# The SSM step sizes behind the convolution, the first loads in another order, and 64 products of a zeroed tile

## The reference, cut to what matters

```python
u = rmsnorm(x, mix_pre_g[0])                      # 256 x 1024
z, xbc, dt = split(u @ w_in, [2048, 5120], -1)    # w_in: 1024 x 5152; dt: 32 columns, the step sizes
xbc = silu(depthwise_conv4(xbc, conv_w) + conv_b) # 3072 channels
xs, bm, cm = split(xbc, [2048, 2560], -1)
dt = softplus(dt + dt_bias);  a = -exp(a_log)     # 32 heads
y = ssd(xs, dt, a, bm, cm)                        # scan; needs cumsum(dt * a)
y = (y + d_skip * xs) * silu(z);  y = grouped_rmsnorm(y) * norm_g;  h = y @ w_out
mem_n = rmsnorm(mem, mem_norm_g)                  # for the cross attention after it
...
```

## Time and profile before

| | us |
|---|---|
| median of 3 runs | 981.83 (981.80 to 982.46) |
| the profiled execution | 982.02 |
| its span, first to last instruction | 980.2 |
| its mean granted TensorE clock | 0.983 of full |

### The profile page before, as it was taken

One profiled execution on the slowest core, in us unless ns is written; L12 is line 12 of the kernel. 1 busy time (PEld: TensorE's weight loads), 2 busy tenths in 40 slices (PEclk: granted clock), 3 DMA queues, 4 the chain that ended last, 5 costly groups with the idle time before them and its releaser, 6 DMA issues.

```text
span 980.2 us, 15470 instructions
## 1 busy us (share of the span) xinstructions
PE 927.5 (95%) x6560; PEld 855.4 (87%) x6560; DVE 562.7 (57%) x644; ACT 487.9 (50%) x669; POOL 37.3 (4%) x52
## 2 busy tenths in 40 slices
PE   2899998998999999999999999999999599999996
PEld 2899997876899889999988899997898499999885
DVE  4778654784475475455544755765654645554533
ACT  4555747773464564443343644665645534444332
POOL 1000001220000000000000021000000000000000
PEclk9899999998999999999999999999999799999999
DMA  9465553223464265555555697433543445555551
GB/s 294 141 194 187 172 173 109 88 86 131 170 221 166 86 215 172 178 195 183 172 188 198 197 275 236 131 129 123 198 152 98 139 133 193 188 171 175 201 181 43
DMA packets 120917, 163.80 MB, mean 167 GB/s; under 512 B 4060, under 2 KB 106644, under 8 KB 120868
## 3 DMA queue, kind: packets, MB, share of 16 engines
q1 hardware_dynamic: 117396, 151.47, 47.4%
q0 software_dynamic: 3472, 11.63, 4.0%
HBM read 162.01 MB, written 1.07 MB: 166 GB/s over the span
## 4 chain that ended last, share of the span: by engine, by line
PE 85%; DVE 7%; ACT 3%; DMA 2%; issue 2%; SPq 0%; POOL 0%; DVEq 0%
PE bank L433 77%; DMA w_raw<-in_ssm_w_in_dram 2%; DVE w_lo L1110 2%; DVE ntmp L1171 1%; PE bank L713 1%; PE bank L684 1%; DVE x L1174 1%; PE bank L533 1%; DVE ntmp L1150 1%; ACT ntmp L822 1%; PE bank L610 1%; PE bank L768 1%; DVE stats L1139 0%; DVE stats L1141 0%; PE bank L758 0%
## 5 line engine op out<-in xcount | busy, mean ns | idle before, releaser
L1110 DVE TENSOR_TENSOR w_lo<-w_raw,w_hi 128x2048 fp32r<-128x2048 f32 x136 | 310.8, 2290 | 229.2 <-ACT w_hi L802 229.1
L433 PE MATMUL bank<-actT_hi,w_hi 128*128 128x256 f32 x1280 | 365.5, 286 | 4.7 <-DVE dtc L1217 2.0
L433 PE MATMUL bank<-actT_lo,w_hi 128*128 128x256 f32 x1280 | 363.8, 284 | 0.0
L433 PE MATMUL bank<-actT_hi,w_lo 128*128 128x256 f32 x1280 | 363.6, 284 | 0.0
L802 ACT ACTIVATE w_hi<-w_raw 128x2048 fp32r<-128x2048 f32 x136 | 258.7, 1907 | 118.3 <-DMA w_raw<-in_ffn_w_down_dram 54.8
L433 PEld LDWEIGHTS bank<-actT_hi,w_hi 128*128 128x128 f32 x1280 | 247.3, 193 | 6.5 <-issue 4.2
L433 PEld LDWEIGHTS bank<-actT_lo,w_hi 128*128 128x128 f32 x1280 | 247.4, 193 | 0.1
L433 PEld LDWEIGHTS bank<-actT_hi,w_lo 128*128 128x128 f32 x1280 | 247.3, 193 | 0.0
L433 PE MATMUL bank<-w_lo,hT_hi 128*128 128x512 f32 x176 | 70.2, 399 | 0.0
L433 PE MATMUL bank<-w_hi,hT_hi 128*128 128x512 f32 x176 | 69.4, 394 | 0.0
L433 PE MATMUL bank<-w_hi,hT_lo 128*128 128x512 f32 x176 | 69.0, 392 | 0.0
(11 more groups left out here) (208 smaller groups left out, 1300.7 us busy)
## 6 DMA issues: line engine op xcount, KB each, us to landing
w_raw<-in_ffn_w_gu_dram SPq DMA_DIRECT2D x44, 1024.0 KB, 5.1
w_raw<-in_ffn_w_down_dram SPq DMA_DIRECT2D x22, 1024.0 KB, 4.9
w_raw<-in_ssm_w_in_dram SPq DMA_DIRECT2D x20, 1024.0 KB, 5.3
w_raw<-in_mem_w_kv_dram SPq DMA_DIRECT2D x16, 1024.0 KB, 5.6
w_raw<-in_ssm_w_out_dram SPq DMA_DIRECT2D x8, 1024.0 KB, 4.9
w_raw<-in_mem_w_q_dram SPq DMA_DIRECT2D x8, 1024.0 KB, 5.2
w_raw<-in_mem_w_o_dram SPq DMA_DIRECT2D x8, 1024.0 KB, 4.9
w_raw<-in_w_kv_dram SPq DMA_DIRECT2D x8, 1024.0 KB, 5.7
```

Source lines behind the costliest of these rows:

```text
L433: ins = pe.matmul(dst, a, b, start=first and n == 0, stop=last and n == len(passes) - 1, skip_group_check=True)
L1110: dve.tensor_tensor(lo[:, s, :], raw[:, s, :], hi[:, s, :].bitcast(F32), ALU.subtract).then_inc(w_lo_done, 1)
```

## The change

- **SP's order** becomes x (two), `pre_row` (taken from POOL), the identity alone (64 KB of the constants), unit 0, the four small parameter loads, unit 1, the rest of the constants, units 2 and 3, `dtw`, then units 4 onward.
- **POOL** waits until the first half of u is written before it loads the dt rows and the table, and until three units are used before the 2 MB of memory gain, `mem` and `post_row`.
- **TensorE** first waits for a zeroed tile (`cum3`, bfloat16), then multiplies it 40 times with 256 columns, then needs the identity only; 24 more such products follow the transposes of the parameters. The first 40 and the 24 are loops (`WARM`). Unit 0 no longer waits for `dt_biased`.
- **The step sizes**: `dtw_hi` and `dtw_lo` are made after the convolution loop; the 24 matmuls stand behind z0, the two transposes behind z1 (banks 6 and 7), `turn(1)` waits for `dt_biased`. ScalarE's table load, memory statistics and the Abs, Exp, Ln, Exp, Ln chain move together to behind the Silu of z2, VectorE's part with them.
- **Unit 0** is made in halves on ScalarE and VectorE. ScalarE's first change of table stands between units 0 and 1. VectorE does the constants (L1193 to L1199) after unit 1's lo instead of ahead of the turn, and waits for the parameters before the turn.
- With one bank entry fewer, `z` and later units swap banks 0 and 1. The buffers from `phase` on move up by 96 bytes, to a multiple of 128.

```diff
+WARM = [10, 6]
...
-BANKED = [("params", 0), ("dt", 0)] + [n for n in NAME_OF if KIND[n[0]] != "M"]
+BANKED = [("params", 0)] + [n for n in NAME_OF if KIND[n[0]] != "M"]
...
+        phase = -(-at[0] // 128) * 128
...
+        dt_heads = place("dt_heads", [P, S], F32, phase + 44544)
...
             for t in range(ST):
                 sp.dma_start(x[:, t, :], A["x"][0, t * P:(t + 1) * P, :]).then_inc(x_loaded[t], 16)
-            sp.dma_start(const[:], A["consts"][:, 0:C_HOT]).then_inc(const_loaded, 16)
+            sp.dma_start(pre_row[:], every_row(TURN_GAIN[0])).then_inc(pre_first, 16)
+            sp.dma_start(const[:, 0:P], A["consts"][:, 0:P]).then_inc(ident_loaded, 16)
+            load(0)
             sp.wait_ge(par_cleared, 1)
             sp.dma_start(par_rows[0:TAPS * CT, 0, :], A["ssm_conv_w"][0].rearrange("k (c p) -> (k c) p", p=P)).then_inc(par_loaded, 16)
             sp.dma_start(par_rows[0:CT, 1, :], A["ssm_conv_b"][0].rearrange("(c p) -> c p", p=P)).then_inc(par_loaded, 16)
             sp.dma_start(par_rows[G_ROW:G_ROW + XT, 1, :], A["ssm_norm_g"][0].rearrange("(c p) -> c p", p=P)).then_inc(par_loaded, 16)
             sp.dma_start(d_pair[D_ROW:D_ROW + XT, :], A["ssm_d"][0].rearrange("(c e) -> c e", e=2)).then_inc(par_loaded, 16)
-            sp.dma_start(dtw[:], row_tiles(w_in, 0, KD, DI + CONV, SSM_HEADS)).then_inc(par_loaded, 16)
-            for u in range(NUNITS):
+            load(1)
+            sp.dma_start(const[:, P:C_HOT], A["consts"][:, P:C_HOT]).then_inc(const_loaded, 16)
+            for u in range(2, SLOTS):
+                load(u)
+            sp.dma_start(dtw[:], row_tiles(w_in, 0, KD, DI + CONV, SSM_HEADS)).then_inc(dtw_loaded, 16)
+            for u in range(SLOTS, NUNITS):
                 load(u)
...
-            pool.dma_start(pre_row[:], every_row(TURN_GAIN[0])).then_inc(pre_loaded, 16)
+            pool.wait_ge(u_ready, 1)
...
             pool.wait_ge(u_ready, 2)
+            pool.wait_ge(w_used, 3)
             pool.dma_start(pre_row[:], every_row(TURN_GAIN[1])).then_inc(pre_loaded, 16)
 
             pool.dma_start(memV[:], mem_t).then_inc(mem_loaded, 16)
...
-            pe.wait_ge(const_loaded, 16)
+            def warm(n):
+
+                with pe.Fori(0, n):
+                    for _ in range(4):
+                        pe.matmul(bank[:, 2, 0:S], cum3[:, 0:P], cum3[:, 0:S], start=True, stop=True, skip_group_check=True)
+
+            pe.wait_ge(zeros_made, 1)
+            warm(WARM[0])
+            pe.wait_ge(ident_loaded, 16)
             turn(0)
...
             pe.wait_ge(consts_made, 1)
             for r in range(2):
-                ins = pe.transpose(bank[:, 0, r * P:(r + 1) * P], par_rows[:, r, :], ident)
+                ins = pe.transpose(bank[:, 3, r * P:(r + 1) * P], par_rows[:, r, :], ident)
             ins.then_inc(par_turned, 1)
+            warm(WARM[1])
             turn_done(0)
...
-            pe.wait_ge(dtw_lo_done, 1)
-            for k in range(KD):
...
+            def steps():
+
+                pe.wait_ge(dtw_lo_done, 1)
+                for k in range(KD):
+                    ins = product(bank[0:SSM_HEADS, 6, 0:S],
+                                  [(dtw_hi[:, k, :], actT_hi[:, k, :]), (dtw_hi[:, k, :], actT_lo[:, k, :]), (dtw_lo[:, k, :], actT_hi[:, k, :])],
+                                  k == 0, k == KD - 1)
+                ins.then_inc(dt_mm, 1)
+
+            def steps_turned():
+
+                pe.wait_ge(dt_copied, 1)
+                for t in range(ST):
+                    ins = pe.transpose(bank[:, 7, t * SSM_HEADS:(t + 1) * SSM_HEADS], dt_heads[0:SSM_HEADS, t * P:(t + 1) * P],
+                                       ident[0:SSM_HEADS, 0:SSM_HEADS])
+                ins.then_inc(dt_turned, 1)
...
             u0 = U[("xbc", 0)]
-            pe.wait_ge(dt_biased, 1)
-            pe.wait_ge(t_out["dve"], 1)
...
+                pe.wait_ge(const_loaded, 16)
                 pe.wait_ge(dt_ready, 1)
...
-                banked("z", i, actT_hi, actT_lo, FREED[V_OF[("z", i)] - 4] if i < 2 else None)
+                banked("z", i, actT_hi, actT_lo, FREED[V_OF[("xbc", 9)]] if i < 2 else None)
+                if i == 0:
+                    steps()
+                if i == 1:
+                    steps_turned()
                 if i == 3:
+                    pe.wait_ge(dt_biased, 1)
                     turn(1)
                 if i == 4:
...
-            act.wait_ge(par_loaded, 80)
-            act.activation(dtw_hi[:], dtw[:], ACT.Copy).then_inc(dtw_hi_done, 1)
             turn(0, actT_hi)
+            hi_part(0, 0)
+            hi_part(0, 1)
+            act.preload_act_table_set("silu_and_others")
             hi_upto(1)
...
+            act.wait_ge(t_out["dve"], 1)
...
             done[0] = U[("z", 0)] + 2
+            act.wait_ge(dtw_loaded, 16)
+            act.activation(dtw_hi[:], dtw[:], ACT.Copy).then_inc(dtw_hi_done, 1)
...
                 hi_upto(U[("z", i)] + 2)
+                if i == 1:
+                    act.wait_ge(dt_mm, 1)
+                    act.activation(dt_heads[0:SSM_HEADS, :], bank[0:SSM_HEADS, 6, 0:S], ACT.Copy).then_inc(dt_copied, 1)
                 act.wait_ge(w_used, U[("z", i)] + 1)
...
-                if i == 1:
+                if i == 2:
...
+                    act.wait_ge(dt_biased, 1)
+                    own.mark(act.activation(dtc[:, 2], dtc[:, 1], ACT.Abs))
...
+                    act.activation(dt_row[:, 1, :], dt_row[:, 1, :], ACT.Exp).then_inc(dt_logged, 1)
                     act.wait_ge(dt_ready, 1)
                     act.activation(dtc[:, 3], dtc[:, 4], ACT.Ln).then_inc(dt_ln, 1)
...
+                elif u == 0:
+                    dve.wait_ge((first_hi, w_hi_done)[part], 1)
...
+            dve.memset(one_col, 1.0).then_inc(zeros_made, 1)
...
-            dve.wait_ge(par_loaded, 80)
+            dve.wait_ge(par_loaded, 64)
...
+            dve.tensor_copy(par_rows[d_rows, 1, :].rearrange("c (e n) -> c e n", e=2), d_pair[d_rows, :].unsqueeze(2).broadcast_to([XT, 2, HD])).then_inc(consts_made, 1)
+            turn(0, actT_hi, actT_lo)
+            lo_part(0, 0)
+            lo_part(0, 1)
+            dve.wait_ge(par_turned, 1)
...
+            lo_upto(1)
             dve.wait_ge(const_loaded, 16)
...
+            def steps_biased():
+                dve.wait_ge(dt_turned, 1)
+                dve.wait_ge(rows_loaded, 64)
...
+                dve.tensor_tensor(dtc[:, 1], dt_raw, bias_row, ALU.add).then_inc(dt_biased, 1)
...
+            def steps_ready():
+                dve.wait_ge(dt_logged, 1)
...
             own.n += 2 * per
             done[0] = 14
+            dve.wait_ge(dtw_hi_done, 1)
+            dve.tensor_tensor(dtw_lo[:], dtw[:], dtw_hi[:].bitcast(F32), ALU.subtract).then_inc(dtw_lo_done, 1)
             for i in range(DI // TC):
                 lo_upto(U[("z", i)] + 2)
-                if i == 1:
+                if i == 2:
+                    steps_biased()
                     for t in range(ST):
...
```

More of the change, by code:

```diff
@@ L810, in hi_part @@
                 ins = act.activation(hi[:, u % SLOTS, cols], raw[:, u % SLOTS, cols], ACT.Copy)
+                if u == 0 and part == 0:
+                    ins.then_inc(first_hi, 1)
                 if part:
@@ L928, in _ @@
                         statistic(2 + t, t, memV[:, t, :])
+                    act.wait_ge(dt_biased, 1)
+                    own.mark(act.activation(dtc[:, 2], dtc[:, 1], ACT.Abs))
+                    own.wait()
+                    own.mark(act.activation(dtc[:, 3], dtc[:, 2], ACT.Exp, scale=-1.0))
+                    own.wait()
+                    act.activation(dtc[:, 4], dtc[:, 3], ACT.Ln, bias=one_col)
+                    act.activation(dt_row[:, 1, :], dt_row[:, 1, :], ACT.Exp).then_inc(dt_logged, 1)
                     act.wait_ge(dt_ready, 1)
@@ L1116, in lo_part @@
                 s = u % SLOTS
-                if part == 0:
+                if part == 0 and u:
                     dve.wait_ge(w_hi_done, u + 1)
+                elif u == 0:
+                    dve.wait_ge((first_hi, w_hi_done)[part], 1)
                 ins = dve.tensor_tensor(lo[:, s, cols], raw[:, s, cols], hi[:, s, cols].bitcast(F32), ALU.subtract)
@@ L1233, in _ @@
-            own.wait()
-            for t in range(ST):
-                ins = dve.scalar_tensor_tensor(out=adt3[:, t], in0=dtc[:, 5, t:t + 1, :].broadcast_to([P, 3, SSM_HEADS]), scalar=-1.0,
-                                               in1=dt_row[:, 1:2, :].broadcast_to([P, 3, SSM_HEADS]), op0=ALU.mult, op1=ALU.mult)
-            ins.then_inc(dt_ready, 1)
+            def steps_biased():
+                dve.wait_ge(dt_turned, 1)
+                dve.wait_ge(rows_loaded, 64)
+                own.mark(dve.memset(brows[:, S:3 * P], NEG))
+                bias_row = dt_row[:, 0:1, :].broadcast_to([P, ST, SSM_HEADS])
+                dt_raw = bank[:, 7, 0:ST * SSM_HEADS].rearrange("p (t h) -> p t h", t=ST)
```

(22 more changed lines are left out.)

71 lines of the change are left out of this document (12 added, 59 removed).

## The result

The changed kernel takes 969.35 us (median of 4 runs, 968.44 to 969.64), the kernel before 982.14 beside it: a ratio of 0.9868, interval 0.985 to 0.9885. The gain is 12.8 us where 9.4 was forecast, and the time lies 0.15 under the low end of the range. The profiled execution took 969.12, its span is 967.3 and its mean granted clock 0.986.

A forecast was written before the change was run, and what follows sets the result against it. TensorE, busy 95% of the span, bounds the kernel, so it must begin earlier or do less. 13.9 (head) - 2.8 - 0.15 - 1.6 (z units) = 9.35 off 982.02 gives 972.7, by median 972.5; range 969.5 to 977.0.

The forecast's parts named there:

- the 96 bytes and the swapped banks: Moved buffers and banks: old placing cost ScalarE's Copy nothing, so 0, or a few tenths either way.
- the head: Everything before unit 0: 12.1 us gained, plus 1.79 if unit 0 runs at the full clock level, 13.9 together.
- S: Start of unit 0 on TensorE, forecast at 15.5 us instead of 27.63.
- rival 1 in its mild form: Head's transfers come later: parameters land at 12.8, unit 0 starts at 18.1, kernel takes 975.1; chance 0.20.
- Unit 0's clock: Unit 0 runs at the full clock level, lasting 5.76 us instead of 7.55: 1.79 gained.
- The products: 40 zeroed-tile products before the turn and 24 after: 0 for both loops; transposes alone had raised the clock.
- The turn: Transposes in the head: second half from 10.1 to 11.0 at the full clock level, ending 13.8 at the lower.
- The z units: Additions to TensorE's unbroken stretch: 24 step-size matmuls 2.8 us, `dtw` rounding 0, two small transposes behind z1 0.15.
- The chain behind z2: Memory statistics and step sizes between z2 and z5: z5 begins 16.1 after z2's end, before 14.5; 1.6 us lost.
- Rival 3 (slower): Step-size chain between z2 and z5 delays `dt_ready`; slower kernel if it came after Z + 19.7; chance 0.03.
- the far end of rival 1: Head: unit 1 lands at 22.97 as before, starts 5.9 later, clock falls (1.8): 980.2; chance 0.03.
- from z5 on nothing different from before but the shift: Changed kernel's timeline after z5: expected the same as before, only earlier.

The follow-up runs named there:

- b_al128: Kernel before with only the buffers from `phase` on 96 bytes higher, at a multiple of 128: 975.7 us, ratio 0.9942.
- a_al32: Changed kernel with the buffers from `phase` on back at the old addresses, 32 bytes past a multiple of 128: 974.84 us.
- a_again: Changed kernel unaltered, run again on another occasion beside other versions on one chip: 970.11 us.
- a_par: Changed kernel with the four parameter loads ahead of unit 0 in SP's queue: 968.37 us.
- a_nowarm: Changed kernel without its 64 products of the zeroed tile: 971.49 us.
- b_order: Kernel before with buffers at a multiple of 128 and the new load order (`dtw` still ahead of unit 1), no products or halves: 968.72 us, ratio 0.9863.
- b_early_par: b_early with the small loads, `dtw` among them, ahead of unit 0 in SP's queue: 967.49 us, ratio 0.9844.
- b_early: b_order with ScalarE's copy of the step sizes between the hi of units 0 and 1, VectorE's bias between their lo: 967.68 us, ratio 0.9853.
- a_warm2: Changed kernel with only the 24 products behind the parameters' transposes, the first 40 left out: 970.3 us.
- a_chain: Changed kernel with the Abs to Exp chain ahead of the memory's statistics, `turn(1)` behind z4 and `cumulate` behind z5: 968.69 us.

## Why the prediction was wrong, point by point

- **The step that failed: "the 96 bytes and the swapped banks".** I priced them at 0 or a few tenths by ScalarE's Copy in and out of the moved buffers. That row answers for ScalarE alone. The engine that bounds the kernel reads `hT`, `y` and `oT` there as stationary operand, 816 times, and the mean durations 392 to 412 beside 389 to 395 for `actT` stood in the profile of before, in groups that I did not lay side by side. The term measures 4.9, by the last part of b_al128 and by the medians of the groups; undone in a_al32 it is 5.2. The medians of whole runs, 6.0 and 5.5, also hold landings and falls of the clock. With 4.9 the sum would have been 13.9 - 4.55 + 4.9 = 14.25 and the forecast 967.6: too low by 1.8, because the head was too hopeful. Two errors stood against each other, and that the measured time lies so close under the range is luck.
- **S.** Forecast 15.5, measured 16.91, and 17.63 in a_again. `pre_row` was there at 7.8, not 6.9; the parameters held VectorE until 11.86, where the sum let it go at 10.1. This is rival 1 in its mild form, at about half its price; a_par took the wait away.
- **Unit 0's clock.** 1.79 was forecast, 7.55 - 5.86 = 1.69 measured. Right in the sum.
- **The products.** Their cost was priced at 0, rightly; but the reason given for doing without them was wrong. Rows 15.90 and 18.62 of the earlier trace rows were taken to show that the turn alone raises the clock for what comes after. In a_nowarm, with nothing between turn and unit 0, unit 0 is at the lower level after 3.7 us of idle time, 2.1 us in the median; whether the level had risen and fallen again in that time, or had never risen, no row shows. And the test itself was one throw of several: after the same 18 transposes the matmuls of the step sizes were at the full level from the first in before, b_order and b_early_par, and at the lower one in b_al128 and b_early. For b_al128:

```profile
15.41 0.42 PE L433 MATMUL bank<-actT_hi,dtw_hi 128*32 128x256 f32 x1 [1.32 <-DVE actT_lo L1158]
```

- In a_warm2 nothing but 18 transposes stands ahead of the 24 products; the last two transposes are 0.11 apart, and the products 0.115 from the first on. The rule of the Trainium skill ("TensorE: Matmul & The Clock Gate", Part 4: PE-mode transpose), that the full level doesn't engage for transposes, disagrees with that row and with 15.90 of before; it agrees with b_al128. What decides between them no run here shows.
- **The turn.** Its second half ran at 0.21 for most of its length, 1.69 instead of 1.0. Since VectorE was waiting for `d_pair` meanwhile, part of it was hidden.
- **The z units.** 24 step matmuls: 2.79, forecast 2.8. Ahead of them TensorE waits 0.25 for `dtw_lo`, which had been priced at 0. The two small transposes cost 0.42 (from 94.93, where z1 begins, to 106.87, where z2 ends, are 11.94, and two units take 11.52), forecast 0.15. Together 3.5, forecast 2.95.
- **The chain behind z2.** Z is the end of z2, here 106.87; z5 begins at Z + 16.1 as forecast, Z + 14.5 before. The waits are those named, 0.73 in the turn and 0.31 before z5, ended by the lo. a_chain, without either, has 1.66 less: the 1.6 of the sum.
- **To `cbT`** the sum becomes 9.35 - 1.4 (S) - 0.1 (clock) - 0.6 (z units) = 7.25; measured 7.3. Rival 3 (slower) and the far end of rival 1 did not come. The statement "from z5 on nothing different from before but the shift" is the one that the profile refutes: 5.6 us of gain lie behind `cbT`.
- **What the gain is due to.** I had argued it from unit 0 not waiting for the step sizes. Nearly all of it is had without moving them: in the medians 6.0 with the addresses (b_al128) and 7.0 more with the order of the loads (b_order); in the profiled spans 6.9, of which 4.9 is the address and 2.0 an earlier landing, and 5.0. What is left for moving the step sizes, the halves and the products is -0.6 in the medians and 1.0 in the spans, not told apart from nothing: a_nowarm, with the step sizes moved and the halves but no products, stands 2.8 over b_order, and the products bring 2.1 of it back.
